# Scores ahead of weighted values: one reordering in TensorE's attention loop

## What is computed

```python
logits = einsum('bqgrd,bqkgd->bqgrk', qb, ks) * scale
logits = where(valid[:, :, None, None, :], logits, -inf)
p = softmax(logits, axis=-1)
out = einsum('bqgrk,bqkgd->bqgrd', p, vs)
```

## Time and profile before

| | |
|---|---|
| three executions | 2478.77, 2481.22 and 2485.99 us, median 2481.22 |
| the profiled execution | 2479.94 us; its span, first to last instruction, 2478.1 us |
| mean granted clock of TensorE over the span | 0.952 of 2.4 GHz |
| TensorE busy with matmuls | 2228.6 us (90%) |
| VectorE busy | 1807.9 us (73%) |
| ScalarE busy | 1376.8 us (56%) |
| the attention loop on TensorE | from 574.3 to 756.9 us of the span |

### The profile page before, as it was taken

How to read it: one execution, slowest core, us unless ns; L and a number is a source line. 1 busy time by engine, 2 the same in 40 slices (tenths; PEclk the granted TensorE clock), 3 DMA queues, 4 the chain that set the end, 5 groups by cost and what they waited for, 6 DMA issues and landing times.

```text
span 2478.1 us, 41791 instructions
## 1 busy us (share of the span) xinstructions
PE 2228.6 (90%) x15519; PEld 1808.2 (73%) x15519; DVE 1807.9 (73%) x2070; ACT 1376.8 (56%) x1547; POOL 527.1 (21%) x457
## 2 busy tenths in 40 slices
PE   5689999776997949999999999999999999999993
PEld 4567788665886737777777777777777777778773
DVE  3489999913434376787788788778778778877885
ACT  4362223465653245666666666666666666666665
POOL 1105787481002000211111011021111111102120
PEclk8899999776998969999999999999999999999997
DMA  5001111001002337988888898898898888989997
GB/s 134 17 21 48 46 48 51 22 17 73 1 1 93 118 103 273 329 295 298 324 308 308 303 320 318 283 333 315 282 333 288 308 322 301 316 298 324 317 322 284
DMA packets 253534, 526.47 MB, mean 212 GB/s; under 512 B 32984, under 2 KB 59736, under 8 KB 253116
## 3 DMA queue, kind: packets, MB, share of 16 engines
q1 hardware_dynamic: 240204, 483.27, 54.6%
q0 software_dynamic: 13264, 42.34, 6.6%
HBM read 490.96 MB, written 35.91 MB: 213 GB/s over the span
## 4 chain that ended last, share of the span: by engine, by line
PE 65%; DMA 10%; ACT 7%; DVE 7%; SPq 5%; issue 5%; POOL 2%; ACTq 0%; DVEq 0%; POOLq 0%
PE ps L1703 11%; PE ps L1705 10%; PE ps L1704 10%; DMA e_raw<-in_w_gate_up_dram 9%; PE ps L1402 6%; PE ps L1404 6%; PE ps L1403 6%; PE ps L1710 4%; PE ps L1581 2%; SPq L722 2%; PE ps L1715 1%; DVE e_wlo L2211 1%; PE ps L1572 1%; SPq L724 1%; SPq L723 1%
## 5 line engine op out<-in xcount | busy, mean ns | idle before, releaser
L2211 DVE TENSOR_TENSOR e_wlo<-e_raw,e_whi 128x2048 fp32r<-128x2048 f32 x410 | 927.2, 2285 | 120.7 <-ACT e_whi L1285 118.6
L1285 ACT ACTIVATE e_whi<-e_raw 128x2048 fp32r<-128x2048 f32 x411 | 783.8, 1915 | 368.2 <-PE ps L1705 180.7
L1703 PE MATMUL ps<-e_whi,xh 128*128 128x512 f32 x1088 | 436.6, 401 | 15.0 <-DVE e_wlo L2211 15.0
L1704 PE MATMUL ps<-e_whi,xl 128*128 128x512 f32 x1088 | 425.1, 391 | 0.0
L1705 PE MATMUL ps<-e_wlo,xh 128*128 128x512 f32 x1088 | 424.7, 390 | 0.0
L933 POOL DMA_INDIRECT x_d<-ym,scur x34 | 72.7, 2137 | 924.2 <-ACT ym L1318 903.7
L1703 PEld LDWEIGHTS ps<-e_whi,xh 128*128 128x128 f32 x1088 | 204.5, 188 | 73.5 <-issue 32.5
L1703 PE MATMUL ps<-e_whi,ath 128*128 128x512 f32 x544 | 221.2, 407 | 21.9 <-DVE atl L2239 21.0
L1705 PEld LDWEIGHTS ps<-e_wlo,xh 128*128 128x128 f32 x1088 | 204.7, 188 | 44.3
L1704 PEld LDWEIGHTS ps<-e_whi,xl 128*128 128x128 f32 x1088 | 204.8, 188 | 38.9
L1705 PE MATMUL ps<-e_wlo,ath 128*128 128x512 f32 x544 | 212.6, 391 | 0.0
(11 more groups left out here) (357 smaller groups left out, 3582.6 us busy)
## 6 DMA issues: line engine op xcount, KB each, us to landing
e_raw<-in_w_gate_up_dram SPq DMA_DIRECT2D x275, 1024.0 KB, 6.0
e_raw<-in_w_down_dram SPq DMA_DIRECT2D x136, 1024.0 KB, 7.9
w_raw<-in_w_in_dram SPq DMA_DIRECT2D x20, 512.0 KB, 3.8
xt<-in_x_dram SPq DMA_DIRECT2D x8, 512.0 KB, 3.6
wo_raw<-in_w_out_dram SPq DMA_DIRECT2D x8, 512.0 KB, 6.7
xr<-in_x_dram SPq DMA_DIRECT2D x8, 512.0 KB, 4.3
x_d<-x SPq DMA_DIRECT2D x8, 512.0 KB, 2.6
h_d<-h SPq DMA_DIRECT2D x8, 512.0 KB, 2.8
```

The costliest lines, as they stand in the source:

```text
L1285: nc.scalar.activation(e_whi[:, m % HRING, :], e_raw[:, m % RING, :], ACT.Copy).then_inc(s.e_hi, 1)
L1703: nc.tensor.matmul(dst, a_hi, slot_hi, start=False, stop=False, skip_group_check=True)
L1704: nc.tensor.matmul(dst, a_lo, slot_hi, start=False, stop=False, skip_group_check=True)
L2211: nc.vector.tensor_tensor(e_wlo[:, m % HRING, :], e_raw[:, m % RING, :], e_whi[:, m % HRING, :].bitcast(F32), ALU.subtract).then_inc(s.e_l ...
```

## The change

In TensorE's loop over the units, the scores of unit u+2 are issued ahead of the weighted values of unit u-1, instead of behind them. Waits and operations stay as they are, and no other engine's order is touched.

```diff
@@ -1596,10 +1596,10 @@
             for u in range(NT * HEADS + 1):
                 if u < NT * HEADS:
                     transposes(u)
+                if u + 2 < NT * HEADS:
+                    scores(u + 2)
                 if u >= 1:
                     values(u - 1)
-                if u + 2 < NT * HEADS:
-                    scores(u + 2)
                 if u % HEADS == 3 and u > HEADS:
                     rows_out(u // HEADS - 1)
             rows_out(NT - 1)
```

## The result

The changed kernel takes 2465.70 us (median of five, 2461.80 to 2466.61) where the kernel before takes 2481.93 (median of five). The ratio is 0.9931, with a 95% interval of 0.9916 to 0.9945: faster, by 14 to 21 us. Timed again beside later experiments it took 2462.92 against 2480.61, ratio 0.9935 (0.9922 to 0.9948). Forecast was a gain of 10.7, to 2470.5. One execution of experiment 6 took 2753.46 us at a mean granted clock of 0.776 and is left out of its median.

The account below looks back on a forecast made before the run. In the attention TensorE was taken as the busiest engine, stalled by seven waits for arow. Gain 11.5 less 0.8 for narrow blocks, handovers, exponential and clock at 0, made 10.7 us: 2481.22 to 2470.5, range 2465.2 to 2476.9.

Parts of the forecast that it names:

- The seven waits: TensorE's waits before weighted values for arow at block starts, 9.9 us in 7 pieces, would go; gain 11.5 us.
- The price per wait: At the start of block 7, one wait costs 1.81 us: 1.58 of idle and 0.23 more.
- the sum for block 7: TensorE's work ahead of the values, 4.09 us, covers the 2.86 until arow allows them, with 1.2 to spare.
- The rest in the narrow blocks: In blocks 1 to 3 about 0.5 us of each arow wait remains; loss 0.8, bounds 0 and 1.5.
- The handovers: TensorE's changed succession of scores, transposes and values, 61 times; taken as 0, bounds 4.9 us lost and 2.4 gained.
- The clock: Rise from 1.2 GHz early in the attention, 3 us earlier or later, worth at most 1.5 us either way.
- Rival D: The clock rises at another time; with full clock 6 us earlier, gain 13.7 us, time 2467.5; chance 0.05.
- The waits for the exponential: Transposes waiting for ScalarE's exponential, 4.6 us, would stay; taken as 0, bounds 0 and a gain of 1.
- Rival A: In blocks 1 to 3 arow waits turn into waits for the exponential; gain 7.7 us, time 2473.5; chance 0.14.
- Rivals B: Values behind scores start late, 0.32 us after them; gain falls to 5.8 us, time 2475.4; chance 0.08.
- C: Values start so late behind scores, 0.30 us more per handover, that the kernel is measurably slower, 2488.6; chance 0.04.
- E: TensorE could already take scores past waiting values, so the order changes nothing; time 2481.2; chance 0.03.

Follow-up runs that it names:

- experiment 6: The changed kernel with the high parts of the next block's queries made by GpSimd instead of ScalarE; 2463.21 us, ratio 0.9933 to the kernel before.
- Experiments 4: The kernel before, TensorE's old order kept, with VectorE making arow one head earlier, behind the mask of head 1; 2470.98 us, ratio 0.9947.
- 7: The changed kernel with VectorE making arow one head later, behind the mask of head 3; 2486.23 us, ratio 1.0028 to the kernel before.
- experiment 5: The changed kernel with the old order in turns 8 and 9, at the start of block 1; 2465.92 us, ratio 0.9946 to the kernel before.
- 3: The kernel before with the new order in all turns except 8i and 8i+1, i from 1 to 7; 2483.83 us, again 2480.38, ratio 0.9994 both times.

## Why the prediction was right or wrong

The direction, the mechanism and its place were right; the size was too small. The gain was 16.2 us by the medians (17.7 the second time) and 14.2 by the profiled executions, against 10.7. The median of 2465.7 lies half a microsecond inside the lower end of the range, 2465.2; the ratio of 0.9931 on the median that the forecast started from would be 2464.1, outside it. So the range was too narrow on the side of the gain. Its lower end is also 0.1 off its own terms, which give 2465.1 (2470.5 less 2.4, 1.0, 1.5 and 0.5).

- **The seven waits.** Forecast 11.5 us, measured 11.3 between the transposes at the block starts. The price per wait, idle plus 0.23, held. So did the sum for block 7, with 1.1 us to spare where 1.2 was worked out, and arow at 2.0 us behind the scores. Experiments 4 and 7 show that it is this wait and no effect of earlier scores.
- **The rest in the narrow blocks.** Forecast a loss of 0.8, measured no row of such a wait. In block 2 the values start 2.13 us after the last scores matmul of unit 18 (601.86 to 603.99), 0.15 after arow ends and so just when it lets them. Unit 17's transposes had waited 0.25 for their exponential by then, and what is left of the wait is under 0.1 us, from the end of the last scores matmul at 603.92. The prediction named this cover and counted half of it.

```profile
601.86 0.34 PE L1404 MATMUL ps<-k_hi,q_lo 128*128 128x384 f32 x1
...
602.84 0.55 PE L1572 MATMUL ps<-cst,a_p 128*128 128x128 f32 x3 [0.25 <-ACT a_p L1187]
...
603.15 0.69 DVE L1959 TENSOR_TENSOR arow<-ps,cols 128x512 f32<-128x512 f32 x1
...
603.58 0.34 PE L1404 MATMUL ps<-k_hi,q_lo 128*128 128x384 f32 x1
...
603.99 0.85 PE L1581 MATMUL ps<-vtok,a_t 128*128 128x64 f32 x6
```

- **The handovers.** This is the step that failed: "I take 0, by L1649", with bounds of 4.9 lost and 2.4 gained. The prediction took its value from one of three handovers, scores to values, and that one costs 0.24 (718.47 to 718.71), near the 0.22 of its row. The gain is in another, transposes to scores, and the row for it stood in the prediction: eight transposes with scores behind them in 0.83 against 0.87. It was used as a bound, not as the value. Blocks 2 to 7 together, without their block starts, are 1.6 us shorter, and block 0 0.5; that is 2.2 us measured where the term stood at 0. With block 1 and the block starts at 0.05 a unit it would be 2.5 to 3 us in all, an estimate.
- **The clock.** Taken at 0, with 1.5 either way. It rose 3.5 us earlier in the first trace of the changed kernel and 7 in the second, after the first matmul; in experiment 5 the late rise goes with the one wait in block 1, at 0.8 to 1.7 us. Rival D named this, at 0.05. Taking the clock at 0 is the second term that was too small.
- **The waits for the exponential** nearly stayed: 5.0 and 5.2 against 4.6, a small loss where the bounds were 0 and a gain of 1. Rival A, at 0.14, did not occur. Rivals B and C did not occur either: the price of a handover has the other sign. Nor did E.

By the first trace: 11.3 for the waits with their block starts, and outside these 3.2, of which 1.0 is block 1 with the early clock and 2.2 the other blocks. That makes 14.5, the difference of the attentions; 0.3 of it is lost outside. The prediction's own test, "the forecast is wrong if packed units change their length", pointed at the right place: they did, by 0.05 to 0.06 us each in block 7.

Open: why the medians differ by 16 to 18 where the pairs of traces differ by 14.2 and 15.7. The intervals of the ratios (13.6 to 20.8 us for the first) hold both. Falls of the clock behind stalls, which were seen in two kernels with the seven stalls (3 and 7) and in none without them, would go that way, but neither trace of the kernel before shows one.

## What to carry to other kernels

A wait at the same place in each of a few blocks can be two engines' orders crossing; list what ends it and when, then put independent work of the waiting engine in front, or move the producer by one step. Here either cured it, and both together did not add. When blocks of matmuls are reordered, sum all the handovers of the cycle and take each from the nearest row that has it, for one that looks neutral can be worth as much as a small wait times its count. Look at the granted clock behind every stall: here a stall of 1.1 us in the stretch at 1.2 GHz went with 0.8 to 1.7 us more, and some stalls at 2.4 GHz with 1.5 more, so an edit that only closes gaps may gain more than the gaps.

## What the hardware showed that was not expected

- One wait of 1.1 us, 15 us into the attention, goes with a rise of the granted clock at 22.0 to 22.8 us after the first matmul (six traces), and its lack or shortening with 15.2 to 19.3 (eight traces). Why is open.
- In the three traces of experiments 3 and 7 the clock fell to 1.2 GHz for 3.4 us behind a stall of 1.5 or 2.1 us in block 4, and in two of them behind one of 1.6 or 2.5 us in block 7 too, at about 1.5 us each. Stalls of 1.5 and 1.6 us in the same blocks of the kernel before did not do it in two traces.
- The start of scores behind transposes: with float32 values behind them, eight transposes hold TensorE 0.87 us, with the split scores behind them 0.80. The matmul that follows starts 0.03 us behind the last transpose instead of 0.11.
